# A two-layer hybrid decoder trunk: rope, gates and mask of the attention loops moved to GpSimd, low parts of four weight pieces to VectorE

## The chip, the cores and the metric

The kernel runs on one NeuronCore of a Trainium2 chip. The metric is the device time of one execution in microseconds (us); lower is better. The kernel is written engine by engine: TensorE (PE), VectorE (DVE), ScalarE (ACT), GpSimd (POOL) and SyncE (SP) each have a program of their own, and semaphores order them.

## The reference

Two layers over 256 positions of width 1024, in float32. What the change touches is the attention inside a layer:

```python
for layer in range(DEPTH):
    h = rms_norm(x, ln1_g[layer])
    (a_q, a_ckv, a_kr, i_q, i_k, i_w, b_u, c_q, c_kv, c_gate) = jnp.split(h @ w_in[layer], offsets, axis=-1)
    a_out = dsa_mixer(...)      # 4 heads over the 64 keys that a top-k of an indexer's scores picks
    b_out = s5_mixer(...)       # diagonal state-space model, GELU and GLU
    c_out = nsa_mixer(...)      # 8 heads: compressed, selected and window branches, summed with gates
    mixed = concatenate([rms_norm(a_out), rms_norm(b_out), rms_norm(c_out)])
    x = x + mixed @ w_out[layer]
    x = x + square(relu(rms_norm(x) @ w_up[layer])) @ w_down[layer]
# nsa_mixer:
k_w = partial_rope(k_w, cos, sin)
gate = sigmoid(gate)                                  # (256, 2, 4, 3)
o = gb[..., 0:1] * o_c + gb[..., 1:2] * o_s + gb[..., 2:3] * o_w
# dsa_mixer:
_, sel = lax.top_k(where(key_pos <= t, score, -inf), 64)
```

## The kernel before, in words

**Weights in two parts.** Each large product is done as three products of a high and a low part of its operands. Weights come in pieces of 128x1024 through rings of four buffers. For piece n, SyncE loads `raw` once the low part of piece n-4 is made; ScalarE copies it to the high part `w_hi` (`hi`, L872); the low part `w_lo`, raw minus high, is made by VectorE (`lo`, L1318) or, for pieces 20 to 23, by GpSimd (`lo_out`, L785); then TensorE uses it (`mm3`, L1756). Pieces 0 to 19 are the input projection, 20 to 27 the output projection, 28 and on the MLP.

**The pair loops.** Between pieces 19 and 20 each layer has a loop over ten pairs of heads: 0 to 3 the selected branch of the C heads (with 256 positions every block is selected, so it is causal attention), 4 to 7 their window branch, 8 and 9 the A heads with the top-k mask. A pair takes these steps, each engine working them off in its own program order:
- TensorE: scores of pair p (8 matmuls `pb<-u_zone` or `w_zone`, L1756), then the turning of pair p-3 (6 transposes, L2174), then the values of pair p-4 (8 matmuls `pb<-ptmp`).
- VectorE, slot p: reads the scores of pair p (four custom instructions `sc_zone<-pb,mask`, L1643: scale, mask, minimum of the negated scores), then for pair p-1 the reciprocal of the sums (L1656) and, for C heads, a multiply by the gate (L1659), both 128x4; then the works that the table `between` puts in slot p.
- ScalarE: exponentials of pair p with sums (L1117), then the copy of turned pair p-2 from PSUM (two halves, L1130), then other copies.
- GpSimd: normalises pair p, `pn = ex * cf` (four instructions of 128x128 and 128x256, L796), then, behind some pairs, a low part.

The table `between` on VectorE also holds the 8 rounds of top-8 (`top8_of_rest`, L1515 and L1519: two MAX8, two MATCH_REPLACE) of which layer 1 does five before the loop, the steps of the compressed branch (`c_open1`, `c_gelu`, `c_keys`, `c_max`, `c_probs`), of the SSM's output (`y_cube`, `y_gelu`, `y_glu`), the rope of the window keys and the gates (`keys_w`, `gates`, in slot 0), and the top-k mask (`a_mask`, L1524, in slot 6), which GpSimd then makes causal (two selects, L595 and L806) before pair 8's scores are read. On TensorE, stage 8 holds the SSM's gate product (`glu`), 8 matmuls; stage 1 its near part, which waits for a DMA.

TensorE's program behind the loop: stage 12 turns pair 9, applies pair 8's values and then does piece 20 (`out_first`), which needs the first pair of `h_lo` (L1246, VectorE); pair 9's values and pieces 21 to 27 follow.

## Time and profile before

| | |
|---|---|
| Median of 3 runs | 647.61 us (647.37 to 648.52) |
| The profiled execution: time, span | 646.98 us, 645.2 us |
| TensorE busy | 616.2 us, 96% of the span |
| VectorE, ScalarE, GpSimd busy | 431.1, 361.3, 232.6 us |
| Chain that ended last, by engine | PE 74%, POOL 10%, DVE 9%, ACT 4% |
| TensorE clock granted | full in nearly all slices |
| Pair loops | about 75 to 121 us and 387 to 432 us |

The rows further down are of four views. Stretches give the busy time of every engine between two times. The chain of waits is followed back from the last instruction: a row is a start, a length and what ran. Rows by time give start, length, engine, line, operation, output and inputs with shapes, the count of merged instructions, and in brackets the idle time before it with what ended that. Times are us from the span's start; a length includes the time that an instruction waits once it has been started.

### The profile page before, as it was taken

To read this page: it belongs to the slowest core of one execution; us is meant where nothing else is said; L and a number is where in the kernel's file an instruction comes from. 1 tells how busy PE (TensorE), PEld (TensorE's weight loads), DVE (VectorE), ACT (ScalarE), POOL (GpSimd) and SP (SyncE) were. 2 spreads that over 40 slices of the span, in tenths; PEclk is the share of its full clock that TensorE was granted. 3 is DMA by queue.
4 is the path that set the end of the run, shared out by engine and by line. 5 is a ranking of instruction groups with operands and counts; after the bars stand their busy time and mean duration, and the time that the engine had idled before them with its cause. 6 is when DMAs were issued, how large, how long until landed. Compare 5 with 4: busy or idle time off the path is not lost.

```text
span 645.2 us, 11319 instructions
## 1 busy us (share of the span) xinstructions
PE 616.2 (96%) x4298; PEld 533.2 (83%) x4298; DVE 431.1 (67%) x796; ACT 361.3 (56%) x672; POOL 232.6 (36%) x403
## 2 busy tenths in 40 slices
PE   7989987999999999999999999799999999999995
PEld 7867865689998899889888787568999899889984
DVE  7698899486655696775576877847765555554553
ACT  6755588746546534443466657984654543553451
POOL 6899258504135999910004204771000000000001
PEclk9999999999999999999999999999999999999998
DMA  9674704155965557476538540323475556656631
GB/s 269 207 202 132 135 3 115 34 172 151 307 197 159 169 173 251 130 227 198 182 96 277 117 129 2 83 67 116 145 259 189 182 188 197 183 175 196 196 99 65
DMA packets 55440, 102.79 MB, mean 159 GB/s; under 512 B 12713, under 2 KB 18906, under 8 KB 55354
## 3 DMA queue, kind: packets, MB, share of 16 engines
q1 hardware_dynamic: 48986, 96.04, 48.4%
q0 software_dynamic: 1792, 4.07, 2.7%
q10 hardware_dynamic: 4608, 1.97, 1.2%
q8 instruction: 34, 0.56, 0.3%
q14 instruction: 20, 0.16, 0.1%
HBM read 99.69 MB, written 1.31 MB: 157 GB/s over the span
## 4 chain that ended last, share of the span: by engine, by line
PE 74%; POOL 10%; DVE 9%; ACT 4%; issue 3%; DVEq 0%; POOLq 0%; ACTq 0%
PE pb L1756 71%; DVE w_lo L1318 2%; POOL rot L605 2%; DVE sc_zone L1643 1%; POOL dtmp L796 1%; POOL yz L605 1%; POOL sp L605 1%; PE pb L1782 1%; DVE dtmp L1519 1%; ACT ptmp L1130 1%; DVE top L1515 1%; ACT tab_zone L1117 1%; PE pb L1910 1%; ACT w_hi L872 1%; POOL rot L619 1%
## 5 line engine op out<-in xcount | busy, mean ns | idle before, releaser
L1318 DVE TENSOR_TENSOR w_lo<-raw,w_hi 128x1024 fp32r<-128x1024 f32 (+2 forms) x176 | 223.5, 1286 | 129.1 <-ACT w_hi L872 128.3
L872 ACT ACTIVATE w_hi<-raw 128x1024 fp32r<-128x1024 f32 (+2 forms) x184 | 187.5, 1027 | 186.3 <-PE pb L1756 171.0
L1756 PE MATMUL pb<-h_hi,w_hi 128*128 128x256 f32 x512 | 145.4, 284 | 0.7 <-DVE w_lo L1318 0.7
L1756 PE MATMUL pb<-h_lo,w_hi 128*128 128x256 f32 x512 | 144.9, 283 | 0.0
L1756 PE MATMUL pb<-h_hi,w_lo 128*128 128x256 f32 x512 | 144.9, 283 | 0.0
L1756 PE MATMUL pb<-w_hi,z_hi 128*128 128x512 f32 x256 | 100.0, 391 | 0.4 <-DVE w_lo L1318 0.4
L1756 PEld LDWEIGHTS pb<-h_hi,w_hi 128*128 128x128 f32 x512 | 98.2, 192 | 2.5 <-issue 1.3
L1756 PE MATMUL pb<-w_hi,z_lo 128*128 128x512 f32 x256 | 99.8, 390 | 0.0
L1756 PE MATMUL pb<-w_lo,z_hi 128*128 128x512 f32 x256 | 99.6, 389 | 0.0
L1756 PEld LDWEIGHTS pb<-h_hi,w_lo 128*128 128x128 f32 x512 | 98.2, 192 | 0.4
L1756 PEld LDWEIGHTS pb<-h_lo,w_hi 128*128 128x128 f32 x512 | 98.2, 192 | 0.0
L1756 PE MATMUL pb<-w_hi,h_hi 128*128 128x512 f32 (+2 forms) x224 | 84.4, 377 | 5.4 <-DVE w_lo L1318 5.2
L1756 PE MATMUL pb<-w_hi,h_lo 128*128 128x512 f32 (+2 forms) x224 | 81.5, 364 | 0.0
L1756 PE MATMUL pb<-w_lo,h_hi 128*128 128x512 f32 (+2 forms) x224 | 81.5, 364 | 0.0
L605 POOL TENSOR_TENSOR tail<-tail 128x1 f32<-128x1 f32 x2 | 0.4, 193 | 172.9 <-ACT proj L1227 172.9
L796 POOL TENSOR_TENSOR dtmp<-tab_zone,cf 128x128 f32<-128x128 f32 x80 | 38.3, 511 | 61.4 <-DVE cf L1659 59.9
L1756 PEld LDWEIGHTS pb<-w_hi,z_hi 128*128 128x128 f32 x256 | 48.1, 188 | 10.5 <-DVE w_lo L1318 0.9
L1756 PEld LDWEIGHTS pb<-w_lo,z_hi 128*128 128x128 f32 x256 | 48.1, 188 | 10.1
L1756 PEld LDWEIGHTS pb<-w_hi,z_lo 128*128 128x128 f32 x256 | 48.1, 188 | 9.4
L1756 PEld LDWEIGHTS pb<-w_hi,h_hi 128*128 128x128 f32 x224 | 42.1, 188 | 14.6 <-DVE w_lo L1318 7.0
L1756 PEld LDWEIGHTS pb<-w_lo,h_hi 128*128 128x128 f32 x224 | 42.1, 188 | 6.6
L1756 PEld LDWEIGHTS pb<-w_hi,h_lo 128*128 128x128 f32 x224 | 42.1, 188 | 5.6
(311 smaller groups left out, 857.0 us busy)
## 6 DMA issues: line engine op xcount, KB each, us to landing
raw<-in_w_up SPq DMA_DIRECT2D x64, 512.0 KB, 3.7
raw<-in_w_down SPq DMA_DIRECT2D x64, 512.0 KB, 4.0
raw<-in_w_in SPq DMA_DIRECT2D x24, 512.0 KB, 4.7
raw<-in_w_out SPq DMA_DIRECT2D x8, 512.0 KB, 3.9
raw<-in_w_out SPq DMA_DIRECT2D x16, 256.0 KB, 4.2
raw<-in_w_in SPq DMA_DIRECT2D x8, 308.0 KB, 3.5
raw<-in_w_in SPq DMA_DIRECT2D x8, 280.0 KB, 2.9
x<-in_x ACTq DMA_DIRECT2D x4, 256.0 KB, 3.8
```

The source lines that it names most:

```text
L605: step(pool.tensor_tensor(o, a, b, op), wait)
L619: return pool.tensor_tensor(os, os, t2, ALU.add)
L796: w = pool.tensor_tensor(pn[:, i, a:b], ex[:, i, a:b], cf[:, i, t:t + 1].to_broadcast([PART, b - a]), ALU.mult)
L872: hi_made.by(act.activation(w_hi[:, n % RING, 0:width(n)], raw[:, n % RING, 0:width(n)], ACT.Copy))
L1117: w = act.activation(ex[:, i, a:b], sc[:, i, a:b], ACT.Exp, scale=-1.0, bias=nmx[:, i, t:t + 1], accum_out=sm[:, i, t:t + 1])
L1130: w = act.activation(pT[:, 2 * (v % 2) + m, :], pb[2 + m][:, 0:384], ACT.Copy)
L1318: lo_made.by(dve.tensor_tensor(w_lo[:, n % RING, 0:width(n)], raw[:, n % RING, 0:width(n)], w_hi[:, n % RING, 0:width(n)].bitcast(F32), AL ...
L1515: step(dve.max(top8[:, c:c + 8], isc[:, a:b]), False)
L1519: step(dve.match_replace(isc[:, a:b], top8[:, c:c + 8], isc[:, a:b], -3e38), False)
L1643: w = dve.tensor_tensor_reduce(sc[:, i, a:b], pb[m][:, a:b], mask[:, a:b], -(HD ** -0.5), 3e38, ALU.add, ALU.min, nmx[:, i, t:t + 1])
L1756: return pe.matmul(o, l, r, start=start, stop=stop, skip_group_check=True)
L1782: return pe.transpose(xT_rows(k, stage)[:, t * PART:(t + 1) * PART], x[:, t, k * PART:(k + 1) * PART], ident[:])
```

## The change

- `keys_w` and `gates` leave VectorE's slot 0 and run on GpSimd ahead of the loop.
- GpSimd's normalisation becomes a TENSOR_SCALAR that takes the factor as a column and, for C heads, the gate as a second column; VectorE's multiply of the reciprocals by the gate goes.
- The mask's threshold runs on GpSimd behind pair 5, behind a new wait for the last round (`topped`).
- The rounds of top-8 are spread anew: in layer 0 slots 0,0,1,2,3,4,4,6 become 0,1,2,3,4,5,6,6; in layer 1 slots 2,4,5 become 0,0,2.
- The low parts of pieces 20 to 23 leave GpSimd (behind pairs 1, 3, 5 and 6) and run on VectorE in slots 8, 10, 11 and 11. ScalarE's high part of piece 20 goes ahead of the loop, those of 21 to 23 behind pairs 1, 3 and 5 (before: 20 to 23 behind 1, 3, 5 and 6).
- ScalarE copies a turned pair in one instruction of 128x768 in place of two of 128x384; for it the eight PSUM banks become one tensor.

```diff
-        HI_OUT = (1, 3, 5, 6)
+        HI_OUT = (None, 1, 3, 5)
...
+                def keys_w():
+
+                    pool.wait_ge(ks_roped.sem, ks_roped.at(L, 1))
+                    pool.wait_ge(tile_sb.sem, tile_sb.at(L, 5))
...
+                    tt(A, kw, c4, ALU.mult, False)
+                    tt(B[:, :, :, 0:HALF], kw[:, :, :, HALF:ROT], s4[:, :, :, 0:HALF], ALU.mult, False)
+                    tt(B[:, :, :, HALF:ROT], kw[:, :, :, 0:HALF], s4[:, :, :, HALF:ROT], ALU.mult)
+                    kw_roped.by(pool.tensor_tensor(kw, A, B, ALU.add))
...
+                keys_w()
+                gates()
                 for p in range(UNITS):
+                    kind, br, b = pairs[p]
...
-                        for t, (a, b) in enumerate(((0, PART), (PART, 384))):
-                            w = pool.tensor_tensor(pn[:, i, a:b], ex[:, i, a:b],
-                                                   cf[:, i, t:t + 1].to_broadcast([PART, b - a]), ALU.mult)
+                        for t, (a, z) in enumerate(((0, PART), (PART, 384))):
+                            pool.nop(nofuse=True)
+                            if kind == "C":
+                                col = 12 * m + 3 * b + 1 + br
+                                w = pool.tensor_scalar(pn[:, i, a:z], ex[:, i, a:z], cf[:, i, t:t + 1],
+                                                       gate[:, t, col:col + 1], ALU.mult, ALU.mult)
+                            else:
+                                w = pool.tensor_scalar(pn[:, i, a:z], ex[:, i, a:z], cf[:, i, t:t + 1], None, ALU.mult)
...
-                    if p in HI_OUT:
-                        lo_out(20 + HI_OUT.index(p))
                     if p == 5:
+                        pool.wait_ge(topped.sem, topped.at(L, 1))
+                        pool.nop(nofuse=True)
+                        a_flag.by(pool.tensor_scalar(abias, isc, -2e38, NEG, ALU.is_gt, ALU.mult))
...
+                hi(L, 20)
                 for p in range(UNITS + 2):
...
-                        for m in range(2):
-                            w = act.activation(pT[:, 2 * (v % 2) + m, :], pb[2 + m][:, 0:384], ACT.Copy)
-                            if m == 0:
-                                step(w, False)
-                        pT_sb.by(w)
+                        pT_sb.by(act.activation(pT[:, 2 * (v % 2):2 * (v % 2) + 2, :], pb_all[:, 2:4, 0:384], ACT.Copy))
...
-                between = {0: [keys_w, gates], 1: [c_open1], 2: [c_gelu], 3: [c_keys], 4: [], 5: [],
+                between = {0: [], 1: [c_open1], 2: [c_gelu], 3: [c_keys], 4: [], 5: [],
...
-                for p in ((0, 0, 1, 2, 3, 4, 4, 6) if L == 0 else (2, 4, 5)):
+                for p in ((0, 1, 2, 3, 4, 5, 6, 6) if L == 0 else (0, 0, 2)):
                     between[p].append(top)
-                between[6].append(a_mask)
...
+                for n in range(20, 24):
+                    between[(8, 10, 11, 11)[n - 20]].append(lambda n=n: lo(n))
...
-                        w = dve.reciprocal(cf[:, both], sm[:, both])
-                        if kind == "C":
-                            step(w)
-                            w = dve.tensor_tensor(cf[:, both], cf[:, both], gate[:].rearrange("p t (g j n) -> p n j g t", g=2, n=3)
-                                                  [:, 1 + br, b], ALU.mult)
-                        cf_sb.by(w)
+                        cf_sb.by(dve.reciprocal(cf[:, both], sm[:, both]))
...
-                dve.wait_ge(lo_made.sem, lo_made.at(L, 24))
                 lo(24)
```

VectorE at the end of layer 0's loop, before: behind the last score read (L1643) come two reciprocals (L1656) with the SSM's gated output between them, then the h_lo.

```order
L1643 ISA sc_zone,nmx<-pb,dtmp 128x256
L1643 ISA nmx 128x1
L1656 RECIPROCAL cf<-sm 128x4
L1246 SCALAR_TENSOR_TENSOR dtmp<-pb,yz 128x512
L1656 RECIPROCAL cf<-sm 128x4
L1246 SCALAR_TENSOR_TENSOR h_lo<-dtmp,vcol,h_hi 128x256 x2
L1246 SCALAR_TENSOR_TENSOR h_lo<-pb,vcol,h_hi 128x256 x6
```

The same place in the changed kernel (its lines have moved: L1668 is the reciprocal, L1338 the low part).

```order
L1656 ISA sc_zone,nmx<-pb,dtmp 128x256
L1656 ISA nmx 128x1
L1668 RECIPROCAL cf<-sm 128x4
L1266 SCALAR_TENSOR_TENSOR dtmp<-pb,yz 128x512
L1668 RECIPROCAL cf<-sm 128x4
L1338 TENSOR_TENSOR w_lo<-raw,w_hi 128x1024 x3
L1266 SCALAR_TENSOR_TENSOR h_lo<-dtmp,vcol,h_hi 128x256 x2
```

Three low parts now stand between the last reciprocal and the first h_lo.

GpSimd behind pair 5 and 6 of layer 0, before: the two selects of the mask, pair 6, the low part of piece 23, pair 7.

```order
L806 AFFINE_SELECT dtmp<-dtmp 128x128
L796 TENSOR_TENSOR dtmp<-tab_zone,cf 128x128
L796 TENSOR_TENSOR dtmp<-tab_zone,cf 128x256
L796 TENSOR_TENSOR dtmp<-tab_zone,cf 128x128
L796 TENSOR_TENSOR dtmp<-tab_zone,cf 128x256
L785 TENSOR_TENSOR w_lo<-raw,w_hi 128x1024
L796 TENSOR_TENSOR dtmp<-tab_zone,cf 128x128
```

The same place in the changed kernel.

```order
L826 TENSOR_SCALAR dtmp<-dtmp 128x384
L597 AFFINE_SELECT dtmp<-dtmp 128x128
L829 AFFINE_SELECT dtmp<-dtmp 128x128
L816 TENSOR_SCALAR dtmp<-tab_zone,cf,gate 128x128
L816 TENSOR_SCALAR dtmp<-tab_zone,cf,gate 128x256
L816 TENSOR_SCALAR dtmp<-tab_zone,cf,gate 128x128
L816 TENSOR_SCALAR dtmp<-tab_zone,cf,gate 128x256
```

The mask's threshold has come in, the low part has gone, and the gates ride in the normalisation.

## Rows read from the trace of the kernel before

**Rows 1.** Busy us (instructions) of PE, PEld, DVE, ACT, POOL in stretches; then clock, DMA.

```profile
90.00:105.00 15.00, 12.44 (x108) 9.02 (x110) 14.24 (x68) 13.11 (x46) 11.57 (x19) 1.00 0.35 90
...
400.00:415.00 15.00, 12.21 (x108) 8.94 (x105) 12.61 (x63) 13.78 (x46) 11.04 (x16) 1.00 0.32 83
```

**Rows 2.** The chain that ended last: start, us, what.

```profile
97.29 0.63 DVE top L1515 x2
...
120.62 22.55 PE pb L1756 x112
...
431.18 22.53 PE pb L1756 x112
```

**Rows 3.** VectorE in layer 0 by time: start, us, instruction, idle before.

```profile
76.92 0.22 DVE L1239 TENSOR_TENSOR dtmp<-proj,rc 128x64 f32<-128x64 f32 x1
...
78.17 0.62 DVE L1515 MAX8 top<-dtmp 128x8 f32<-128x128 f32 x2
...
81.50 0.28 DVE L1643 CUSTOM_DVE_ANT_0 sc_zone<-pb,cmask 128x128 f32<-128x128 f32 x1
...
82.60 0.17 DVE L1656 RECIPROCAL cf<-sm 128x4 f32<-128x4 f32 x1
82.81 0.17 DVE L1659 TENSOR_TENSOR cf<-cf,gate 128x4 f32<-128x4 f32 x1
...
104.29 0.78 DVE L1524 TENSOR_SCALAR dtmp<-dtmp 128x384 f32<-128x384 f32 x1
```

**Rows 4.** TensorE, layer 0: scores of pair 1, SSM near part, gate product.

```profile
78.09 0.93 PE L1756 MATMUL pb<-u_zone 64*128 64x128 f32 x8
...
81.40 1.08 PE L1756 MATMUL pb<-tk,uu 128*32 128x128 f32 x32 [1.14 <-DMA tk<-rk_hbm]
...
109.51 1.89 PE L1756 MATMUL pb<-dtmp,glw 128*128 128x256 f32 x8
```

**Rows 5.** GpSimd against VectorE, layer 0: a stalled gate multiply.

```profile
110.41 1.94 DVE L1659 TENSOR_TENSOR cf<-cf,gate 128x4 f32<-128x4 f32 x1
...
109.97 2.36 POOL L785 TENSOR_TENSOR w_lo<-raw,w_hi 128x1024 fp32r<-128x1024 f32 x1
```

**Rows 6.** VectorE and GpSimd taking turns in the layer 0 MLP.

```profile
178.00 3.50 DVE L1318 TENSOR_TENSOR w_lo<-raw,w_hi 128x1024 fp32r<-128x1024 f32 x3 [1.28 <-ACT w_hi L872]
...
221.80 20.61 DVE L1318 TENSOR_TENSOR w_lo<-raw,w_hi 128x1024 fp32r<-128x1024 f32 x8
...
183.17 1.07 POOL L610 TENSOR_SCALAR sp<-sp 128x8 f32<-128x8 f32 x1 [0.15 <-POOL sp L609]
...
256.20 1.38 POOL L605 TENSOR_TENSOR rot<-rot 128x120 f32<-128x120 f32 x1
```

**Rows 7.** The end of the loop, layer 0: ScalarE, VectorE, GpSimd, TensorE.

```profile
114.83 0.43 ACT L1117 ACTIVATE tab_zone<-sc_zone,nmx 128x128 f32<-128x128 f32 x1
...
116.74 0.18 DVE L1656 RECIPROCAL cf<-sm 128x4 f32<-128x4 f32 x1 [0.99 <-ACT tab_zone L1117]
118.90 1.35 DVE L1246 SCALAR_TENSOR_TENSOR h_lo<-dtmp,vcol,h_hi 128x256 fp32r<-128x256 f32 x2 [1.99 <-ACT h_hi L1105]
...
117.00 1.90 POOL L796 TENSOR_TENSOR dtmp<-tab_zone,cf 128x128 f32<-128x128 f32 x4 [0.81 <-DVE cf L1656]
...
119.77 0.85 PE L2174 MATMUL pb<-ident,dtmp 128*128 128x128 f32 x6 [0.52 <-ACT ptmp L1130]
...
121.35 0.50 PE L1756 MATMUL pb<-w_hi,h_hi 128*128 128x512 f32 x1
```

**Rows 8.** GpSimd, layer 0: an instruction with one SBUF operand.

```profile
107.24 0.28 POOL L595 TENSOR_SCALAR_AFFINE_SELECT dtmp<-dtmp 128x128 f32<-128x128 f32 x1
```

**Rows 9.** Layer 1: VectorE idle at pair 1, exp of pair 9, last reciprocal.

```profile
393.17 0.29 DVE L1643 CUSTOM_DVE_ANT_0 sc_zone<-pb,cmask 128x128 f32<-128x128 f32 x1 [3.73 <-PE pb L1756]
...
427.31 0.18 DVE L1656 RECIPROCAL cf<-sm 128x4 f32<-128x4 f32 x1 [1.25 <-ACT tab_zone L1117]
...
425.42 0.40 ACT L1117 ACTIVATE tab_zone<-sc_zone,nmx 128x128 f32<-128x128 f32 x1 [0.15 <-POOL dtmp L796]
```

More of the change, by code:

```diff
@@ L290, in trunk @@
         rk_hbm = [nc.dram_tensor(f"rk_hbm{i}", (16, S5_G, PART), F32).ap() for i in range(DEPTH)]
-        pb = [ctx.enter_context(nc.psum_tensor(f"pb{i}", [PART, 512], F32)) for i in range(8)]
+        pb_all = ctx.enter_context(nc.psum_tensor("pb", [PART, 8, 512], F32))
+        pb = [pb_all[:, i] for i in range(8)]
         x_loaded = [sig(f"x_loaded{b}", 0) for b in range(4)]
@@ L351, in trunk @@
         isc_made = sig("isc_made", 1)
+        topped = sig("topped", 1)
         kv_ps = sig("kv_ps", 2)
@@ L1508, in index_sum, with top8_of_rest @@
                     dve.wait_ge(isc_made.sem, isc_made.at(L, 1))
-                def top8_of_rest():
+                def top8_of_rest(last=False):
                     step.all()
@@ L1518, in top8_of_rest @@
                     for a, b, c in ((0, PART, 0), (PART, 384, 8)):
-                        step(dve.match_replace(isc[:, a:b], top8[:, c:c + 8], isc[:, a:b], -3e38), False)
-                def a_mask():
-                    step.all()
-                    a_flag.by(dve.tensor_scalar(abias, isc, -2e38, NEG, ALU.is_gt, ALU.mult))
+                        m = dve.match_replace(isc[:, a:b], top8[:, c:c + 8], isc[:, a:b], -3e38)
+                        if last and c:
+                            topped.by(m)
+                        else:
+                            step(m, False)
                 def y_cube():
@@ L1582, in c_probs @@
                     step(dve.reciprocal(cs[:, 2, :], cs[:, 1, :]))
+                    dve.wait_ge(gate_sb.sem, gate_sb.at(L, 1))
                     by_block = [cs[:, i, :].rearrange("p (t j g) -> p t j g", t=TT, g=2) for i in (1, 2)]
@@ L1586, in c_probs @@
                                                  cs[:, 1, :].unsqueeze(2).to_broadcast([PART, 16, 16]), ALU.mult))
-                def gates():
-                    dve.wait_ge(gate_in.sem, gate_in.at(L, 1))
-                    ts(gate[:], gate[:], 0.5, 0.5, ALU.mult, ALU.add)
-                    c_gate = gate[:].rearrange("p t (h n) -> p t h n", n=3)[:, :, :, 0]
-                    gate_sb.by(dve.tensor_tensor(c_gate, c_gate, cone[:, :, 0:1].to_broadcast([PART, TT, C_HEADS]), ALU.mult))
-                    dve.wait_ge(gate_sb.sem, gate_sb.at(L, 1))
                 top = top8_of_rest
@@ L1599, in keys_s @@
                     keys(4, O_KS, ks_roped)
-                def keys_w():
-                    keys(5, O_KW, kw_roped)
                 if L == 0:
@@ L1626, in _ @@
                     between[p].append(work)
-                for p in ((0, 0, 1, 2, 3, 4, 4, 6) if L == 0 else (2, 4, 5)):
+                for p in ((0, 1, 2, 3, 4, 5, 6, 6) if L == 0 else (0, 0, 2)):
                     between[p].append(top)
-                between[6].append(a_mask)
                 assert 8 * sum(works.count(top) for works in (*behind.values(), *between.values())) == TOPK
+                for n in range(20, 24):
+                    between[(8, 10, 11, 11)[n - 20]].append(lambda n=n: lo(n))
+                last_slot = max(p for p, works in between.items() if top in works)
+                between[last_slot][-1] = lambda: top(True)
                 for p in range(UNITS + 2):
@@ L1650, in _ @@
                         v = p - 1
-                        kind, br, b = pairs[v]
                         both = slice(2 * (v % 2), 2 * (v % 2) + 2)
```

14 lines of the change are left out of this document (9 added, 5 removed).

## The prediction

> **What bounds the kernel now.** I read the stretches first, then the chain of waits, then each engine by time. On the chain TensorE runs in long unbroken pieces: 22.55 us from 120.62 and 22.53 us from 431.18, each right behind a pair loop [rows 2]. Outside the two pair loops (75 to 121 us in layer 0, 387 to 432 in layer 1) the change touches nothing that TensorE waits for. So it is worth what it moves one instruction per layer: the first product of piece 20, which opens the output projection. In layer 0 that is at 121.35 us [rows 7], 0.73 behind the start of the chain's piece; in layer 1 it is 0.73 behind 431.18 too, at 431.91. Every us there is a us at the end.
>
> Inside the loops the stretches show who is short of time [rows 1]. In layer 0, from 90 to 105 us, VectorE is busy 14.2 of 15 us, and the chain runs over its top-8 rounds [rows 2]. In layer 1, from 400 to 415, VectorE is at 12.6 and ScalarE at 13.8 of 15: four engines wait for each other in turn, and no single one binds.
>
> **Layer 0, up to the exponentials of pair 9.** Rope and gates take VectorE from 76.92 to 78.17, 1.25 us, and two rounds of top-8 follow, 3.3 us, before pair 1's scores are read at 81.50 [rows 3]. Now there is no rope and one round, so VectorE is free by 78.6. TensorE gives pair 1's scores from 78.09, in 0.93 us [rows 4], and with the signal they can be read at 79.2. That is a lead of 2.3. Pair 2 stands on TensorE behind the SSM product that waits for a DMA until 81.40 and lasts 1.08 [rows 4]; it is read at 83.5, where it was at 85.7, and the lead stays.
> From there, slot by slot on VectorE, with a round at 1.4 to 1.6. A multiply by the gates costs 0.2: it must wait for the reciprocal and starts 0.21 after it [rows 3], where the slot's next work would have started at once. Slot 4 loses one of two rounds, and waits a little for the tanh that was hidden: lead 3.2 at pair 5. Slot 5 gains a round and loses a multiply: 2.0 at pair 6. Slot 6 holds two rounds where it held one and the mask, 0.78 long [rows 3]: 1.5 at pair 7. Slot 7 loses a multiply that stalled behind GpSimd's low part, 1.2 in all: 2.7 at pair 8. Behind pair 8's scores TensorE has the SSM gate product, 1.89 us [rows 4], ahead of pair 9's scores; it follows earlier work of TensorE, which comes 1.9 sooner. So the lead at pair 9 is 1.9, and through ScalarE's copy and tanh the exponentials of pair 9, at 114.83 before [rows 7], come at 112.9: a lead of **2.0**.
> What else the change moves here costs nothing. ScalarE's single copy of a turned pair saves it a few hundredths each time. Its copy of piece 20, a little over 1 us, falls where it waits for pair 0's scores; the raw piece was asked for ten us earlier. Rope and gates on GpSimd fall between 73 and 77 us, when it has no work: its first multiply of the loop comes behind the reciprocal of pair 0. TensorE wants these keys just after 79. Were the cover gone, they would cost GpSimd's own 2 us there.
>
> **Layer 1, up to the same point.** VectorE idles 3.73 us before pair 1 [rows 9], and the two rounds moved there, about 3.0, fit in. Up to pair 4 nothing comes earlier, since TensorE and ScalarE hold the pace. Slots 4 and 5 lose a round each: leads of 0.9 at pair 5, limited by a tanh, and 2.4 at pair 6. Then the compressed probabilities wait for ScalarE, whose own row of work is not shorter (1.5 at pair 7). With the mask early and pieces 22 and 23 gone from GpSimd, pairs 8 and 9 keep 1.6 to 2.3. The exponentials of pair 9 were at 425.42, released by GpSimd [rows 9]; I expect them at 423.5, a lead of **1.9**.
>
> **The end of the loop, both layers.** From the last reciprocal to piece 20 it is 4.61 us in layer 0, 116.74 to 121.35 [rows 7], and 4.60 in layer 1, from 427.31 [rows 9]. Behind the reciprocal VectorE idled until the h_lo at 118.90, and GpSimd normalised pair 9 in 1.90 [rows 7]. Now the low parts of pieces 21, 22 and 23 stand straight behind the reciprocal. Each reads two SBUF tensors; so do the two h_lo behind them, and GpSimd's four instructions read SBUF as well. The trace shows what happens then. VectorE's 128x4 multiply lasted 1.94 us and ended when GpSimd's low part did, at 109.97 + 2.36 [rows 5]. The other way round, a TENSOR_SCALAR of GpSimd of 128x8 took 1.07 and a 128x120 product 1.38, when a free one of 128x128 takes 0.28 [rows 6, 8]. And eight low parts took 20.61 us beside GpSimd's long products where three took 3.50 beside short ones [rows 6]: strict turns, one instruction each.
> In turns, counted from the reciprocal's start, with a low part at 1.14 (3.50 less the last one's 0.09, by 3 [rows 6]): first low part to 1.23; GpSimd's first 128 columns to 1.39; second low part to 2.53; 256 columns to 2.84; third to 3.98; 128 columns to 4.14; first h_lo (half of 1.35, [rows 7]) to 4.78; last 256 columns and their signal to 5.23. Then TensorE turns pair 9 and applies pair 8's values, 0.80 each: piece 20 at **6.83**, 2.2 us later than before.
> For an instruction of GpSimd that has waited I count 0.16 and 0.31 beyond the wait, about 0.17 less than its whole length. No row shows a TENSOR_SCALAR of this width. Its bounds are the select of one operand, 0.28 for 128 columns [rows 8], and the product that it replaces, 1.90 for a pair [rows 7]; I take 0.33 and 0.48, nearer the select, as it too reads one tensor. At the product's length the end comes 0.4 later in each layer.
> The Trainium skill ("GPSIMD Engine Reference", Engine selection) calls two-input elementwise work on GpSimd about twice as slow as on VectorE, but one-input work roughly line rate. By that the end would come about 0.1 us earlier in each layer than I count.
>
> **Sum.** Layer 0: -2.0 + 2.2, about +0.2. Layer 1: -1.9 + 2.2, +0.3. Together **+0.5 us**: the profiled execution's 646.98 becomes 647.5. The median of the runs is 647.61, so I say 648.1. The loads of pieces 24 to 27 now start some ten us later, each behind a low part, but they are first wanted five us after piece 20 starts, and the first of them is asked for ten us before that: nothing. Piece 21 waits for h_lo that follow the last turned pair, and moves with it.
>
> **Rivals.** 0.2% is 1.3 us, about what a measurement of this kernel tells from no change.
> *Faster: the turns at the end are cheaper than that.* If pair 9's normalisation is not held up, VectorE alone sets piece 20, at 0.09 + 3 x 1.14 + 1.35 = 4.9 behind the reciprocal instead of 4.6. The layers then gain 2.0 - 0.3 and 1.9 - 0.3, 3.3 us in all: 644.3. The loops may gain more than my walk has as well, since the stall of rows 5 is one of several. For it: VectorE's gain is sure, the turns are inferred from other stretches. Against it: rows 6 show no exception. Chance 0.34 for all beyond 1.3 us.
> *Slower: GpSimd's new form is slow.* The factor now comes through a pointer. At 0.5 and 0.8 for 128 and 256 columns the end grows by 1.1 us a layer, 2.2 in all: 650.3. It decides from about 0.1 us an instruction over my figure; in mid-loop GpSimd has over 1 us a slot to spare, so the end alone shows it. For it: nothing bounds it in the trace. Against it: the last two pairs need one factor only. Chance 0.28.
> The Trainium skill (same page, Performance pitfalls) has small separate reads at about 102 cycles of 1.2 GHz each; were a pointer such a read, the time would be 0.7 us over my sum. No row here shows it.
> *It doesn't do what it says.* The rounds stay eight and three; if something else than VectorE paces layer 0, its lead stays under 1 us while both ends pay 2.2, and the time is 649.5. I count this with the slower case.
>
> **Numbers.** Forecast, within 1.3 us of before: 0.38, at 648.1 us. The range, 645.0 to 650.6, leaves out the far part of the faster case and the tail of the slower one.
>
> **What would show it.** Layer 0: pair 1's scores read near 79.2, exponentials of pair 9 near 112.9; layer 1: near 423.5. That is the loops' part. The end's part: pair 9's normalisation stretched to 5 us from the reciprocal, with low parts of VectorE between its instructions, and piece 20 near 121.6 and 432.2. If its four instructions take under 2.5 us, I am wrong to the fast side; if a mid-loop pair takes GpSimd over 2 us, to the slow side. A lead under 1 us at pair 9 of layer 0 would mean that VectorE did not pace it.

## The result, and the profile after

| | before | changed |
|---|---|---|
| Median, 6 runs each | 647.7 us (646.97 to 648.82) | 652.88 us (651.29 to 655.08) |
| Profiled execution: time, span | 646.98, 645.2 | 655.08, 653.3 |
| Mean granted clock of the profiled execution | 0.997 | 0.984 |

The change makes the kernel slower: ratio 1.0082, 95% interval 1.0068 to 1.0095, some 5.2 us. The profiled execution of the changed kernel is the slowest of its six; the account below is of that one, 8.1 us longer in span than the one of before. Times and ratios in this document are of executions in the chip's fast state; one execution of one kernel further down was in its slower state and is left out.

The chain of waits of the changed kernel, where it passes the two loops' ends (start, us, what):

```profile
74.93 7.71 DMA tk<-rk_hbm
...
113.20 3.00 POOL dtmp L819 x4
...
116.32 5.67 POOL dtmp L819 x4
...
122.03 1.54 PE pb L2180 x6
...
123.58 24.48 PE pb L1762 x112
...
429.99 5.55 POOL dtmp L819 x4
...
435.58 1.54 PE pb L2180 x6
437.13 24.66 PE pb L1762 x112
```

In [rows 2] the pieces of TensorE behind the loops were 22.55 and 22.53 us long. They are 24.48 and 24.66 now, for the same 112 matmuls, and GpSimd's normalisations of pairs 8 and 9 (L819) stand on the chain in front of them. So the loss has two parts: a later start of this piece, and a longer piece. The second shows in the stretches of TensorE (busy us, matmuls, granted clock, DMA share, GB/s):

```profile
118.00:120.00 2.00, 0.41 (x6) 1.00 0.63 165
120.00:122.00 2.00, 0.00 (x0) 0.73 1.06 231
122.00:124.00 2.00, 1.97 (x10) 0.50 1.06 246
...
126.00:128.00 2.00, 2.00 (x7) 0.57 0.00 1
128.00:130.00 2.00, 2.00 (x14) 1.00 0.00 0
```

TensorE was busy 0.41 us from 118 to 120 and not at all to 122. Near 121, inside this pause, its granted clock fell to 0.5, the 1.2 GHz level, and it came back between 127 and 128. Pair 9's transposes took 1.54 us where they took 0.85 in [rows 7]. Layer 1 shows the same: the clock fell between 434.5 and 435 and came back between 441.5 and 442 us. The execution of before had a clock of 1.00 in every stretch of both loops.

VectorE and GpSimd in layer 0, by time, against [rows 3, 6, 7]:

```profile
79.80 0.29 DVE L1656 CUSTOM_DVE_ANT_0 sc_zone<-pb,cmask 128x128 f32<-128x128 f32 x1 [0.62 <-PE pb L1762]
...
115.94 0.18 DVE L1668 RECIPROCAL cf<-sm 128x4 f32<-128x4 f32 x1 [1.00 <-ACT tab_zone L1141]
116.04 3.55 DVE L1338 TENSOR_TENSOR w_lo<-raw,w_hi 128x1024 fp32r<-128x1024 f32 x3
119.52 1.09 DVE L1266 SCALAR_TENSOR_TENSOR h_lo<-dtmp,vcol,h_hi 128x256 fp32r<-128x256 f32 x2
```

```profile
105.04 1.53 POOL L826 TENSOR_SCALAR dtmp<-dtmp 128x384 f32<-128x384 f32 x1 [0.94 <-DVE dtmp L1539]
...
113.20 8.78 POOL L819 TENSOR_SCALAR dtmp<-tab_zone,cf 128x128 f32<-128x128 f32 x8 [0.81 <-DVE cf L1668]
```

The last reciprocal comes at 115.94 instead of 116.74. Three low parts follow it in 3.55 us, and the eight instructions of pairs 8 and 9 on GpSimd last 8.78 us instead of two times 1.90. ScalarE's exponentials of pairs 8 and 9 of layer 0, then the high part of piece 20 and pairs 0 and 9 of layer 1:

```profile
110.54 0.40 ACT L1141 ACTIVATE tab_zone<-sc_zone,nmx 128x128 f32<-128x128 f32 x1 [1.93 <-POOL dtmp L816]
...
114.05 0.42 ACT L1141 ACTIVATE tab_zone<-sc_zone,nmx 128x128 f32<-128x128 f32 x1
...
394.16 1.06 ACT L895 ACTIVATE w_hi<-raw 128x1024 fp32r<-128x1024 f32 x1
395.11 0.40 ACT L1141 ACTIVATE tab_zone<-sc_zone,nmx 128x128 f32<-128x128 f32 x1
...
427.61 0.41 ACT L1141 ACTIVATE tab_zone<-sc_zone,nmx 128x128 f32<-128x128 f32 x1
```

**The account.** Each row is the change against the execution of before, in us. In layer 1 the lag of 4.89 that layer 0 leaves is taken off, which supposes that it is carried along unchanged.

| | layer 0 | layer 1 |
|---|---|---|
| Last reciprocal | -0.80 (116.74 to 115.94) | -2.70 (427.31 to 429.50, less 4.89) |
| From it to the transposes of pair 9 | +3.06 (3.03 to 6.09) | +3.06 (3.02 to 6.08) |
| From these to the end of TensorE's piece | +2.63 (23.40 to 26.03) | +2.83 (23.38 to 26.21) |
| Together | +4.89 | +3.19 |

The two layers make 8.1, the spans' difference. The third row is the same work of TensorE at a lower clock for a part of it.

### The profile page after: what moved, and what is told of

Same layout as the page of the kernel before. It is cut to its first block, busy times and chain, and to the rows that moved or that the text cites. A ratio compares the mean times of both kernels' runs of the same rounds, so it can differ in the third digit from the quotient of the medians.

```text
span 653.3 us, 11283 instructions
## 1 busy us (share of the span) xinstructions
PE 622.4 (95%) x4298; PEld 537.4 (82%) x4298; DVE 427.5 (65%) x774; ACT 360.0 (55%) x652; POOL 234.2 (36%) x409
## 4 chain that ended last, share of the span: by engine, by line
PE 75%; POOL 10%; DVE 5%; ACT 3%; DMA 2%; issue 2%; SPq 1%; POOLq 0%; DVEq 0%; ACTq 0%
PE pb L1762 72%; POOL dtmp L819 3%; DVE w_lo L1338 2%; POOL sp L607 1%; POOL rot L607 1%; DMA tk<-rk_hbm 1%; POOL yz L607 1%; PE pb L2180 1%; ACT w_hi L895 1%; DVE sc_zone L1656 1%; PE pb L1788 1%; PE pb L1916 1%; DMA proj<-in_ln_g 1%; SPq L452 1%; ACT tab_zone L1141 1%
## 5 line engine op out<-in xcount | busy, mean ns | idle before, releaser
L1338 DVE TENSOR_TENSOR w_lo<-raw,w_hi 128x1024 fp32r<-128x1024 f32 (+2 forms) x184 | 232.7, 1282 | 130.4 <-ACT w_hi L895 129.7
L1762 PE MATMUL pb<-w_hi,h_hi 128*128 128x512 f32 (+2 forms) x224 | 86.4, 386 | 4.6 <-DVE w_lo L1338 4.4
L1762 PE MATMUL pb<-w_hi,h_lo 128*128 128x512 f32 (+2 forms) x224 | 83.2, 371 | 0.0
L1762 PE MATMUL pb<-w_lo,h_hi 128*128 128x512 f32 (+2 forms) x224 | 82.9, 370 | 0.0
L816 POOL TENSOR_SCALAR dtmp<-tab_zone,cf,gate 128x128 f32<-128x128 f32 x64 | 33.3, 538 | 28.2 <-DVE cf L1668 28.2
```

What stands on the lines that cost most here:

```text
L816: w = pool.tensor_scalar(pn[:, i, a:z], ex[:, i, a:z], cf[:, i, t:t + 1], gate[:, t, col:col + 1], ALU.mult, ALU.mult)
L1338: lo_made.by(dve.tensor_tensor(w_lo[:, n % RING, 0:width(n)], raw[:, n % RING, 0:width(n)], w_hi[:, n % RING, 0:width(n)].bitcast(F32), AL ...
L1762: return pe.matmul(o, l, r, start=start, stop=stop, skip_group_check=True)
```

## The experiments

Sixteen kernels were timed, each beside the kernel before on the same chip, and one of them twice; there are 5 to 12 executions of each. The chip is not the same for all, so two of these kernels are best compared by their ratios. A lead below is taken against the profiled execution of before; TensorE's pause and clock are those of the one profiled execution.

### First: undo one suspect at a time

**The low parts back on GpSimd.**

```diff
+                    if p in (1, 3, 5, 6):
+                        lo_out(20 + (1, 3, 5, 6).index(p))
...
-                for n in range(20, 24):
-                    between[(8, 10, 11, 11)[n - 20]].append(lambda n=n: lo(n))
```

> The changed kernel with the low parts of pieces 20 to 23 back on GpSimd behind pairs 1, 3, 5 and 6, all else as changed. Theory A (turns, then the clock): the three low parts behind the last reciprocal lengthen the last normalisation by turns over the memory port, the pause that this makes on TensorE lets its granted clock fall to a half, and both are gone here: from the last reciprocal to piece 20 some 4.6 and 4.0 us again in the two layers instead of 7.6, granted clock 1.00 from 115 to 130 us, the twelve normalisations of an instruction of pairs 8 and 9 near 0.4 and 0.6 us, time 644 to 647 us (the leads of the loop, 1.5 and 2.7 us, less something for GpSimd, which carries 9.5 us more again). Theory B (form): a multiplication by one column of numbers is itself slow on GpSimd (1.1 us in pairs 8 and 9): these stay near 1.1 us, the end of the loop stays 2 us longer than before a layer, time 649 to 652. Theory C (the loop gained nothing): time 647.5 to 648.5 with the clock at 1.00.

650.02 us (647.68 to 654.58), ratio 1.0037 (1.0017 to 1.0058). The four instructions of pair 9 took 3.0 us although no low part ran beside them, so the one column is slow by itself, as in theory B, and the time is in its range; the pause at pair 9's transposes was 1.24 us and the clock stayed up there. But it fell at another place, from about 414 to 417 us, behind a pause of 1.92 us for a DMA, and the mean clocks of the twelve runs go from 0.997 to 0.982, with the slowest run at the lowest.

**The low parts earlier on VectorE**: `between[(6, 7, 8, 9)[n - 20]].insert(0, ...)` in place of `(8, 10, 11, 11)`.

> The changed kernel with VectorE's low parts of pieces 20 to 23 ahead of the other work of rounds 6, 7, 8 and 9, so that none is behind the last reciprocal. Theory A: recip to piece 20 near 4 us, clock at 1.00, each low part costs VectorE 1.2 us in rounds where it has up to 1.7 us idle in layer 0: time 643.5 to 646.5. Theory B (form): the single-column instructions of pairs 8 and 9 stay near 1.1 us, end of the loop 2 us longer than before, time 648 to 651. Theory C: 647.5 or more with the clock at 1.00.

649.44 us (646.95 to 651.34), ratio 1.0026 (1.0009 to 1.0044). The single column took 0.92 us for 256 columns here too, with no low part behind the last reciprocal. In layer 0 the low parts lengthened TensorE's pause before pair 8's scores from 1.6 to 2.73 us, and the clock fell at 107. Not theory A alone: the form costs too, and VectorE had no room in slot 6.

**TensorE kept at work in the pause.**

```diff
+                def keep_up():
+
+                    pe.wait_ge(b_made.sem, b_made.at(L, 1))
+                    run_up(10)
...
-                           3: [c_second], 4: [c_scores], 5: [], 6: [], 7: [], 8: [], 9: [], 10: [], 12: [out_first]}
+                           3: [c_second], 4: [c_scores], 5: [], 6: [], 7: [], 8: [], 9: [], 10: [], 11: [keep_up], 12: [out_first]}
```

`run_up(10)` is ten matmuls of the unit matrix with itself, into a bank that nothing reads then.

> The changed kernel with ten matmuls of the unit matrix (128 columns, into a bank that nothing reads then) on TensorE between the output of pair 7 and the transposes of pair 9, some 2.9 us of work in a pause of 3.6 us; the low parts stay where the change has them. If the clock fell because TensorE stood still, and its fall cost 2 us a layer: granted clock 1.00 (or a fall of under 1 us) from 120 to 130 and 435 to 445 us, transposes of pair 9 near 0.85 us instead of 1.54, 112 matmuls of the output projection in 22.5 instead of 24.5 us, time 648 to 650. If the fall has another cause (the power of the half before, or a coincidence): clock 0.5 there again, time 652 to 654.

649.27 us (646.95 to 655.72), ratio 1.0027 (1.0005 to 1.0050): 3.6 us less than the changed kernel, with nothing of its waits removed. TensorE at the end of layer 0's loop, by time, and then its piece in the chain of waits:

```profile
116.52 2.50 PE L1762 MATMUL pb<-ident 128*128 128x128 f32 x20
120.22 0.88 PE L2185 MATMUL pb<-ident,dtmp 128*128 128x128 f32 x6 [1.21 <-POOL dtmp L819]
...
121.09 22.53 PE pb L1762 x112
```

The ten matmuls (20 instructions) took 2.50 us. The transposes still waited for GpSimd and started at 120.22, 6.09 behind the last reciprocal as before this edit, but took 0.88 instead of 1.54, and the 112 matmuls behind them 22.53 instead of 24.48 (22.53 instead of 24.66 in layer 1). The clock was at 1.00 at both loops' ends. Single executions still reach 655.72, with a mean clock of 0.986; where the clock fell in them, no trace shows.

**The normalisation of two tensors again.** GpSimd `tensor_tensor(pn, ex, cf[...].to_broadcast(...))` for all pairs, VectorE's multiply by the gate back.

> The changed kernel with the normalisation as a multiplication of two tensors again (the factor's column repeated) and the gate multiplied in by VectorE; rope, gates and mask stay on GpSimd, the low parts on VectorE behind the last pairs. Theory A: the form does not matter (0.45 to 0.51 and 0.63 us with two columns against 0.41 and 0.61 of two tensors in the traces), VectorE's gate multiplications cost some 0.2 us a pair where nothing stalls them: last normalisation still 5 to 5.7 us, clock at a half again, time 652 to 654. Theory B (form): the last normalisations fall to 2 to 3 us, the clock stays up, time 646 to 649.

651.43 us (647.79 to 654.28), ratio 1.0057 (1.0040 to 1.0074). Pair 9 took 4.93 us beside the low parts instead of 5.67, the pause was 2.78 instead of 3.63. In the profiled execution, the fastest of the twelve, the clock held after that pause in both layers and fell instead between 105 and 106, after one of 2.14 us. The time, outside both ranges, lies between theory A's and theory B's: the form is a part of the loss and not the whole.

### Then: each cost by itself

**Only pairs 8 and 9 of two tensors** (the `else` branch of L819 alone).

> The changed kernel with one thing undone: the normalisation of pairs 8 and 9, which have no gate, multiplies two tensors again in place of a tensor by one column; pairs 0 to 7 keep the two columns, the low parts stay behind the last pairs. The traces so far give 1.96 us for four instructions with two columns, 1.90 for four of two tensors, and about 3.0 us for four with a single column even where no low part runs beside them. If the single column is the slow form: last normalisation 4.9 us beside the three low parts (5.67 and 5.55 in the changed kernel), pair 8's near 1.9 to 2.8 instead of 3.0, TensorE's pause before the last transposes 2.8 instead of 3.6 us, so at times no fall of the clock there, time 649.5 to 651.5. If the length is all of the low parts' making: no change, 652 to 654.

649.27 us (646.07 to 651.64), ratio 1.0024 (1.0006 to 1.0043). As expected for a slow single column: 1.90 for pair 8, 4.93 for pair 9, pause 2.79. The clock fell after it in both layers.

**The kernel before with the low parts moved alone** (and the high parts, which go ahead of them).

```diff
-        HI_OUT = (1, 3, 5, 6)
+        HI_OUT = (None, 1, 3, 5)
...
-                    if p in HI_OUT:
-                        lo_out(20 + HI_OUT.index(p))
...
+                hi(L, 20)
...
+                for n in range(20, 24):
+                    between[(8, 10, 11, 11)[n - 20]].append(lambda n=n: lo(n))
```

> The kernel before with one part of the change alone: the low parts of pieces 20 to 23 made by VectorE behind the last pairs (and their high parts a pair earlier, as in the change). Normalisation of two tensors, gates, rope and mask on VectorE. If the low parts behind the last reciprocal are the loss: the last normalisation goes from 1.90 to 4.9 us, TensorE's pause before it to 2.8 us, with the clock falling in most executions; GpSimd's 9.5 us of low parts a loop are gone, and so is the stalled gate multiplication of 1.94 us, worth 0.5 to 1.5 us a layer: time 649.5 to 652. If they are harmless: 645 to 647.

653.50 us (653.09 to 653.85), ratio 1.0089 (1.0076 to 1.0103). This one part makes a loss as large as the whole change (ratio 1.0082), and larger than was expected of it. The end of layer 0's loop, VectorE, GpSimd and TensorE:

```profile
116.37 0.18 DVE L1649 RECIPROCAL cf<-sm 128x4 f32<-128x4 f32 x1 [0.99 <-ACT tab_zone L1108]
...
116.63 4.93 POOL L788 TENSOR_TENSOR dtmp<-tab_zone,cf 128x128 f32<-128x128 f32 x4 [1.28 <-DVE cf L1649]
...
121.61 1.54 PE L2166 MATMUL pb<-ident,dtmp 128*128 128x128 f32 x6 [2.72 <-POOL dtmp L788]
```

The last reciprocal is 0.37 us earlier than in [rows 7]. The normalisation takes 4.93 instead of 1.90, TensorE pauses 2.72, and its transposes run at half clock; the clock fell at both ends of the loops.

**The rest alone**: low parts on GpSimd and normalisation of two tensors, both as before; rope, gates and mask on GpSimd, the rounds spread.

> The changed kernel with both suspects undone: low parts on GpSimd behind pairs 1, 3, 5 and 6, and the normalisation of two tensors with VectorE's gate multiplication, as before. Left of the change: rope, gates and mask on GpSimd, the maxima spread, one copy of the transposed factors. If the loop's gain is in these: exp of pair 9 1.5 to 2 us earlier in each layer, last reciprocal to piece 20 4.6 and 4.0 us, 644 to 646 with the clock up. If the gain needs GpSimd free of low parts: exp of pair 9 within 0.7 us of before, 646.5 to 648.5. Falls of the clock in the loop would lift the median over that by 1 to 2 us.

647.62 us (645.78 to 651.01), ratio 1.0005 (0.9991 to 1.0018): no difference that can be measured. With 9.5 us of low parts a loop still on GpSimd the exponentials of pair 9 came at 115.31 us in layer 0, no lead at all. The low parts moved alone bring 0.37 us there. The lead needs both, the moved work and a GpSimd without low parts.

**The kernel before with a longer last normalisation.**

```diff
+                    if p == UNITS - 1:
+                        for m in (0, 1, 0):
+                            i = 2 * (p % 2) + m
+                            for t, (a, b) in enumerate(((0, PART), (PART, 384))):
+                                step(pool.tensor_tensor(pn[:, i, a:b], ex[:, i, a:b],
+                                                        cf[:, i, t:t + 1].to_broadcast([PART, b - a]), ALU.mult))
```

> The kernel before with one addition: GpSimd does six of the instructions of the last normalisation once more ahead of it, the same products into the same places, so that it ends some 3.3 us later a layer and TensorE pauses 3.8 us there instead of 0.5. Nothing of the change is in it. If a pause of this length is itself what lets the granted clock fall: clock at a half from about 121 us and again from 435 us in most executions, transposes of pair 9 at up to 1.54 us, median 655.5 to 658. If the fall has another cause in the change: 653.5 to 654.5, clock 1.00.

656.91 us (655.91 to 660.19), ratio 1.0146 (1.0114 to 1.0179), 9.5 us, though the transposes came only 2.8 us later a layer, 5.6 in all. The transposes of pair 9 and the stretches around them:

```profile
122.45 1.35 PE L2180 MATMUL pb<-ident,dtmp 128*128 128x128 f32 x6 [3.33 <-POOL dtmp L802]
```

```profile
120.00:122.00 2.00, 0.00 (x0) 1.00 0.00 0
122.00:124.00 2.00, 1.55 (x8) 0.68 0.00 0
124.00:126.00 2.00, 2.00 (x10) 0.50 0.00 0
```

So a pause alone, without low parts beside it, new forms or moved work, is followed by the fall; it came after both loops. The DMA share is 0.00 here, so the transfers that ran in the changed kernel's pause (1.06) are not needed for it either. The pause is charged twice: once as a wait and once in the work behind it.

### The same work, with the low parts behind the normalisation

```diff
-                for n in range(20, 24):
-                    between[(8, 10, 11, 11)[n - 20]].append(lambda n=n: lo(n))
+                between[8].append(lambda: lo(20))
...
-                h_rest(8, gm[:, L], out_rows, K_ORDER)
+                dve.wait_ge(pn_sb.sem, pn_sb.at(L, UNITS))
+                for i, (first, count) in enumerate(((0, 2), (2, 4), (6, 2))):
+                    lo(21 + i)
+                    h_rest(8, gm[:, L], out_rows, K_ORDER, first, count)
```

The first version of this had the counts 2, 2, 4, with pairs 8 and 9 of two tensors:

> The changed kernel with pairs 8 and 9 as a multiplication of two tensors, and the low parts of pieces 21, 22 and 23 behind the end of the last normalisation, between the low parts of h, instead of beside it (piece 20's stays in round 8). If both costs of the end of the loop are named rightly (turns with the low parts, the single column): last normalisation 1.9 us, last reciprocal to piece 20 4.0 to 4.7 us as before the change, no pause of TensorE over 1.3 us there, and what is left is the lead of the loop, 1.5 and 2.7 us: 643.5 to 645 where the clock stays up, and a median up to 2 us above that if the clock falls in the pause before pair 8's scores (1.6 us at 104.4) in some executions. If the low parts are then late for pieces 21 and 22: PE waits for w_lo, 646 to 648.

645.28 us (643.39 to 647.70), ratio 0.9961 (0.9945 to 0.9976): faster than both kernels. TensorE still waited 1.12 us a layer for an `h_lo` behind piece 23's low part. With the counts above:

> The version with the low parts behind the last normalisation (pairs 8 and 9 of two tensors), with the low parts of h for the fourth to sixth column block ahead of piece 23's low part instead of behind it. In the version before, TensorE waited 1.12 us in each layer for a low part of h behind that piece; if that wait is all that stood there, it goes, and nothing else changes: 2.2 us less in both layers, 643 to 644 us median. If the low part of piece 23 is then late in its place, or ScalarE's high parts of h come no earlier: 644.5 to 645.5.

642.93 us (641.18 to 643.85), ratio 0.9918 (0.9891 to 0.9944). The end of layer 0's loop, VectorE, GpSimd, TensorE:

```profile
113.34 0.18 DVE L1668 RECIPROCAL cf<-sm 128x4 f32<-128x4 f32 x1 [1.00 <-ACT tab_zone L1142]
115.54 1.73 DVE L1339 TENSOR_TENSOR w_lo<-raw,w_hi 128x1024 fp32r<-128x1024 f32 x1 [2.02 <-POOL dtmp L819]
117.19 0.87 DVE L1267 SCALAR_TENSOR_TENSOR h_lo<-dtmp,vcol,h_hi 128x256 fp32r<-128x256 f32 x2
...
113.60 1.91 POOL L819 TENSOR_TENSOR dtmp<-tab_zone,cf 128x128 f32<-128x128 f32 x4 [1.22 <-DVE cf L1668]
...
116.26 0.85 PE L2183 MATMUL pb<-ident,dtmp 128*128 128x128 f32 x6 [0.45 <-ACT ptmp L1154]
...
118.11 0.50 PE L1765 MATMUL pb<-w_hi,h_hi 128*128 128x512 f32 x1 [0.21 <-DVE h_lo L1267]
```

VectorE waits for GpSimd's end and makes its low parts then, beside TensorE's work. From the last reciprocal to piece 20 it is 4.77 us in both layers, against 4.61 and 4.60 in [rows 7, 9]; the last reciprocal itself comes 3.4 us earlier in layer 0 and, by the same measure as above, 2.7 in layer 1. The clock stood at 1.00 in both loops. Run again beside the last kernel below, this version gave 642.44 us (641.15 to 645.01), ratio 0.9924 (0.9906 to 0.9943):

> The fastest version so far (pairs 8 and 9 of two tensors, low parts behind the last normalisation, piece 23's behind the sixth block of h) once more, unchanged, beside the run with the constant on the same chip: 642.9 us median again, within 1 us.

**With matmuls before pair 7's scores** (four of the unit matrix, 1.2 us, in layer 0's stage 6).

> As the version with piece 23's low part behind the sixth block of h, and in layer 0 four matmuls of the unit matrix (128 columns, 1.2 us) in TensorE's pause of 1.6 us before the scores of pair 7. If falls of the clock after that pause are what spreads the times of a shortened loop (643.4 to 647.7 us for its parent): same median or up to 1 us less, spread under 2 us. If not: same median and the same spread.

643.03 us (641.17 to 646.15), ratio 0.9927 (0.9901 to 0.9954): nothing gained, and a spread of 5 us. But the matmuls do not run where they were meant to. TensorE by time:

```profile
99.33 1.16 PE L1765 MATMUL pb<-ident 128*128 128x128 f32 x8
...
104.88 0.93 PE L1765 MATMUL pb<-w_zone 64*128 64x128 f32 x8 [1.49 <-DVE nmx L1656]
```

The pause of 1.6 us stands before pair 8's scores (`w_zone`), and the work of stage 6 comes before pair 7's. So the four matmuls ran at 99.33, and the longer pause stayed, at 1.49 us. Whether falls of the clock behind it spread the shortened loop's times was not tested.

### What GpSimd's TENSOR_SCALAR costs

All of these have the low parts behind the normalisation; the first has the counts 2, 2, 4.

> The version with the low parts of pieces 21 to 23 behind the last normalisation (645.28 us median), but pairs 8 and 9 with the single-column multiplication of the change. Nothing else runs on the memory port then, so this prices the form alone: four instructions 3.0 us instead of 1.90, 1.1 us a layer on the path from the last reciprocal to piece 20 (pair 8's is partly beside TensorE's other work): 647.5 to 648.5. If the form costs only beside low parts: 645 to 646.

646.59 us (645.34 to 651.29), ratio 0.9987 (0.9968 to 1.0006), between its two expectations and 1.3 above its parent (0.9961); the two intervals overlap, so the price is read from the instructions. Groups of GpSimd in layer 0 (busy us, mean ns of one):

```profile
L819 POOL TENSOR_SCALAR dtmp<-tab_zone,cf 128x256 f32<-128x256 f32 x4 | 3.7, 930 | 0.0
L819 POOL TENSOR_SCALAR dtmp<-tab_zone,cf 128x128 f32<-128x128 f32 x3 | 1.8, 609 | 0.1
```

> The fastest version so far (low parts behind the last normalisation, piece 23's behind the sixth block of h, 642.93 us median) with pairs 8 and 9 as a multiplication by two columns: the product with the factor, then its minimum with the same factor, which changes nothing since an exponential is at most 1. If a single column is the slow form as such: 0.45 us for 128 and 0.56 for 256 columns as in the pairs with a gate, 2.0 us for the last normalisation, time 642.5 to 643.5. If pairs 8 and 9 are slow with any TENSOR_SCALAR: 0.61 and 0.93 us, 3.1 for the four, 644 to 645.5.

650.36 us (648.28 to 655.16), ratio 1.0051 (1.0033 to 1.0070), above both expectations:

```profile
L819 POOL TENSOR_SCALAR dtmp<-tab_zone,cf 128x256 f32<-128x256 f32 x4 | 4.8, 1212 | 0.0
L819 POOL TENSOR_SCALAR dtmp<-tab_zone,cf 128x128 f32<-128x128 f32 x4 | 3.2, 792 | 0.8 <-DVE cf L1668 0.8
```

> The same, with the single column and, as second operation, a maximum with the constant 0.0, which changes nothing either. If what is slow is leaving the second operation out: 2.0 us for the last normalisation, 642.5 to 643.5. If it is every form in which not both operands are columns (the mask's threshold with two constants took 1.53 us for 128x384, 4.0 ns a column, where two columns of numbers take 2.2): 3.1 us, 644 to 645.5.

649.04 us (646.62 to 654.51), ratio 1.0030 (1.0008 to 1.0051), above both too:

```profile
L819 POOL TENSOR_SCALAR dtmp<-tab_zone,cf 128x256 f32<-128x256 f32 x4 | 4.6, 1140 | 0.0
L819 POOL TENSOR_SCALAR dtmp<-tab_zone,cf 128x128 f32<-128x128 f32 x4 | 2.9, 721 | 0.8 <-DVE cf L1668 0.8
```

The last normalisation is 2.1 us longer in the first and 1.7 in the second than with two tensors. Twice that, 4.1 and 3.5 us, is a part only of the 7.4 and 6.1 us that their medians lie above that kernel. In the first, the clock also fell behind the pause of 2.26 us in layer 1; what the rest is was not traced.

Neither the number of columns nor the missing second operation explains the price; the fast groups of the changed kernel, 97 to 104 us, have two columns and multiply twice:

```profile
L816 POOL TENSOR_SCALAR dtmp<-tab_zone,cf,gate 128x256 f32<-128x256 f32 x4 | 2.2, 559 | 0.0
L816 POOL TENSOR_SCALAR dtmp<-tab_zone,cf,gate 128x128 f32<-128x128 f32 x4 | 1.8, 452 | 3.9 <-DVE cf L1668 3.9
```

So the last kernel of this series keeps one column and multiplies by 1.0: `tensor_scalar(pn, ex, cf[:, i, t:t + 1], 1.0, ALU.mult, ALU.mult)`.

> The fastest version so far with pairs 8 and 9 as one column and a multiplication by the constant 1.0. The runs so far have four instructions of a pair at 1.96 us (two columns, multiply and multiply), 3.0 (one column, nothing behind it), 3.6 (one column, maximum with 0.0) and 3.9 (two columns, multiply and minimum). If the pair of operations decides and multiply with multiply is the fast one: 2.0 us for the last normalisation, time 642.5 to 643.8, as with two tensors. If a constant in the place of the second column is slow: 3.0 us or more, 644.5 to 650.

642.44 us (641.36 to 645.58), ratio 0.9922 (0.9901 to 0.9943), the time of two tensors:

```profile
L819 POOL TENSOR_SCALAR dtmp<-tab_zone,cf 128x256 f32<-128x256 f32 x4 | 1.9, 481 | 0.0
L819 POOL TENSOR_SCALAR dtmp<-tab_zone,cf 128x128 f32<-128x128 f32 x4 | 1.5, 374 | 2.3 <-DVE cf L1668 2.3
```

The same product of 256 columns costs 930 ns with nothing behind the multiply and 481 ns with a multiply by 1.0 behind it. With the rows above, the pair of operations sets the price.

### The mask's threshold back on VectorE

> The version with the constant 1.0 (642.44 us median) and the mask's threshold back on VectorE in slot 6, as before the change; GpSimd keeps the two selects. In layer 0 the threshold takes GpSimd 1.53 us behind VectorE's last round, the normalisation of pair 6 starts only behind it, and ScalarE waits 1.93 us for it before pair 8's exponentials. If the threshold on GpSimd is what cost layer 0 its lead at pair 8 (2.17 us at pair 7, 0.14 at pair 8 in the changed kernel): the wait of 1.93 shrinks to under 0.8, the interval of 4.5 us between the exponentials of pairs 7 and 8 to 3.3, 1 us less in all: 641 to 641.8. If VectorE's 0.78 us in slot 6 is worth as much: no change, 642 to 643; if it is worth more, 643 to 644.

645.62 us (642.28 to 650.22), ratio 0.9965 (0.9946 to 0.9985), slower than its parent by 3 us and above all three expectations. ScalarE's exponentials of pairs 7, 8 and 9, TensorE, and its stretches:

```profile
105.14 0.40 ACT L1138 ACTIVATE tab_zone<-sc_zone,nmx 128x128 f32<-128x128 f32 x1 [1.11 <-DVE nmx L1653]
...
108.10 0.39 ACT L1138 ACTIVATE tab_zone<-sc_zone,nmx 128x128 f32<-128x128 f32 x1
...
114.75 0.42 ACT L1138 ACTIVATE tab_zone<-sc_zone,nmx 128x128 f32<-128x128 f32 x1
...
105.16 0.93 PE L1762 MATMUL pb<-w_zone 64*128 64x128 f32 x8 [2.15 <-DVE nmx L1653]
106.02 1.33 PE L2180 MATMUL pb<-ident,dtmp 128*128 128x128 f32 x6
```

```profile
104.00:106.00 2.00, 0.84 (x8) 1.00 0.01 4
106.00:108.00 2.00, 2.00 (x12) 0.57 0.00 0
```

The mechanism was as expected: 2.96 us from pair 7 to pair 8 instead of 4.5, and ScalarE's wait for GpSimd is gone. But slot 6 grew on VectorE, TensorE's pause before pair 8's scores went from 1.6 to 2.15 us, the clock fell at 106 and stayed down until 110, and TensorE gave pair 9's scores late: their exponentials start 1.2 us later than in the parent, where pair 8's start 1.9 us earlier. In this execution a gain inside the loop is handed back with the clock; that the median's 3 us come from it is likely and not shown.

## Why the prediction was wrong

**The bound: right in place, wrong in its price.** Piece 20's start decides, and all of the loss is at it or right behind it. But "every us there is a us at the end" counted TensorE's work behind it at the rows of before, all at full clock. The wait that the change makes is followed by matmuls at half clock: +2.63 and +2.83 us in the profiled execution, from transposes to the end of the projection. This is the failed step, and the largest; no term of the sum had it. The kernel with matmuls in the pause gets 3.6 us back: of the median's loss of 5.2 it leaves 1.9, inside the range. And the longer normalisation alone brings the fall about. The other executions of the changed kernel are shorter and have higher mean clocks (0.987 to 0.992, against 0.984), so the fall probably costs less in them; only the profiled one shows where it was.

**The end of the loop, +2.2 a layer.** The turns of the two engines came as forecast: low parts of VectorE between GpSimd's instructions, pair 9 stretched to more than 5 us. The size was off: the transposes would start 5.23 us behind the reciprocal by the sum, and started at 6.09. The term that was mis-sized is the TENSOR_SCALAR, taken as 0.33 and 0.48 us from the select's 0.28 [rows 8] and measured, with nothing beside it, at 0.61 and 0.93. That is outside the upper bound of 1.90 for a pair: 3.0. The slower rival named this form, and its argument against ("the last two pairs need one factor only") was backwards: two columns with two multiplies cost 1.96 a pair, the one factor 3.0. For the same reason the sign that was given for it, a mid-loop pair over 2 us, could not see it: those pairs multiply twice. The rival's own price is a little off as well: 0.17 and 0.32 more, twice each, make 1.0 a layer, not 1.1. With the product of two tensors pair 9 still takes 4.93 us beside the low parts, so of its 5.67 us the form makes 0.74, and the turns make 3.03 over the 1.90 of an undisturbed one. With that product the transposes start 5.24 us behind the reciprocal (120.96 and 115.72), where the sum's own rule for it, 0.4 later, gives 5.6: the walk of the turns was some 0.4 too long, and this hid a part of what the form cost. The rule on one-input work at line rate (the Trainium skill, "GPSIMD Engine Reference", Engine selection) isn't borne out by these rows: the mask's threshold of 128x384, one input, takes GpSimd 1.53 us and VectorE 0.78 [rows 3], and one factor on 256 columns takes GpSimd 930 ns, longer than the two-input product's 614.

**The loops, leads of 2.0 and 1.9.** Pair 1 was read at 79.80 against 79.2, in an execution that was already 0.6 us behind at 65 us, after a fall of the clock at 12 us. The exponentials of pair 9 came at 114.05 in layer 0, a lead of 0.8 (112.9 was expected); 427.61 in layer 1 is 422.7 without layer 0's lag, a lead of 2.7 (423.5 was expected). Together 3.5 against the 3.9 of the sum, and that is luck: layer 0 fell short by 1.2, and layer 1 brought 0.8 more than was forecast. A lead under 1 us in layer 0 was the sign that VectorE did not pace it, and behind pair 7 GpSimd did. Inside layer 0 two steps failed. The threshold of the mask was given to GpSimd at no cost: it took 1.53 us, pair 6's normalisation stood behind it, ScalarE waited 1.93 us for that, and a lead of 2.17 at pair 7 was 0.14 at pair 8, where 2.7 was forecast. The SSM's near product waited for its DMA (the chain's first row) until 82.68 instead of 81.40; in the profile of the version with the low parts behind the normalisation it waited for no DMA, and the exponentials of pair 9 came at 111.45, a lead of 3.4; so the profile of one run undersells the loop. In layer 1 the high part of piece 20, also counted at nothing, stood 0.95 us in front of pair 0's exponentials; in spite of it layer 1's lead came out larger than forecast.

**The numbers.** 647.5 for the profiled execution needed both ends at +2.2; with +3.06 for each end and the clock's 2.63 and 2.83 the same sum gives 654.7, against 655.08. The range ended at 650.6 because the slower case held only the form's price. A cause that acts after the wait was in none of the cases.

## What to carry to other kernels

A wait in front of dense TensorE work can cost more than its length: look at the granted clock behind the longest pause, and if a change lengthens one, add a term for the work behind it at the slower level. Where two engines take turns, as VectorE's low parts and GpSimd's normalisation do here (1.90 us alone, 4.93 beside them), the work that can wait belongs behind the step that everyone waits for, even if its engine is idle now. Three low parts 2 us later, spread among the `h_lo`, with the last pairs' form changed, turned 5 us lost into 4.5 to 5 us gained. Price an instruction by a row with the same operations, not only the same engine, operands and shape.

## What the runs showed of the hardware

- TensorE's granted clock fell to a half in or behind pauses of 1.9 to 3.6 us, but not behind each. A pause of 2.14 us was followed by a fall in one kernel (the normalisation of two tensors) and not in another (the moved work alone). One of 2.26 was followed by it in layer 1 and not in layer 0 of one execution. Pauses of 2.78 and 2.79 passed without. The pause's length alone does not tell; what else decides was not found.
- GpSimd's TENSOR_SCALAR on 128x256 float32, one column, by its operations: multiply and multiply 481 ns (by the constant 1.0) or 547 to 559 (by a second column), multiply alone 930, multiply and maximum with a constant 1140, multiply and minimum with a column 1212. The product of two tensors took 614. In other shapes: the mask's threshold, a comparison and a multiply with two constants on 128x384, took GpSimd 1530 ns and VectorE 780.
- A normalisation of four instructions that took GpSimd 1.90 us alone took 4.93 beside three low parts of VectorE, 3.55 us long together, in three kernels and both layers alike.
